# 160 tokens gathered in place of 128 in the expert stage of a two-block model, with dense products of 352 columns

## The reference, cut to what matters

```python
q = (hb @ wq).reshape(128, 8, 2, 128)                      # 8 heads, two halves
s = einsum('thsd,snd->thsn', q, subkeys)                   # 128 scores for each half
s1, i1 = top_k(s[:, :, 0], 16); s2, i2 = top_k(s[:, :, 1], 16)
sc, ci = top_k(s1[..., None] + s2[..., None, :], 16)       # 16 best of 256 pairs
idx = e1 * 128 + e2                                        # 8*16 = 128 experts of 16384 for each token
gate = softmax(sc)
act = gelu(einsum('td,thkd->thk', hb, u_tab[idx])) * gate
out = einsum('thk,thkd->td', act, v_tab[idx])
```

## Time and profile before

| what | value |
|---|---|
| median of 3 runs | 4420.25 us (4418.15 to 4424.22) |
| the profiled execution | 4425.3 us, its span 4423.5 us |
| TensorE busy | 4248.9 us, 96% |
| VectorE, ScalarE, GpSimd busy | 3004.6, 1804.8 and 1455.6 us (68%, 41%, 33%) |
| chain that ended last | PE 79%, DVE 11%, ACT 3%, issue 3%, POOL 2%, DMA 2% |

### The profile page before, as it was taken

How to read it: one execution, slowest core, us unless ns; L and a number is a source line. 1 busy time by engine, 2 the same in 40 slices (tenths; PEclk the granted TensorE clock), 3 DMA queues, 4 the chain that set the end, 5 groups by cost and what they waited for, 6 DMA issues and landing times.

```text
span 4423.5 us, 66804 instructions
## 1 busy us (share of the span) xinstructions
PE 4248.9 (96%) x26227; PEld 3705.3 (84%) x26227; DVE 3004.6 (68%) x5041; ACT 1804.8 (41%) x2815; POOL 1455.6 (33%) x992
## 2 busy tenths in 40 slices
PE   7979999999999999999999999999999999999998
PEld 5856755779999999999989877699889877877997
DVE  5866657559767868788778446488378544655873
ACT  4245421233335653333355355355255333324542
POOL 2044224314885437778621110212111110112121
PEclk8989999999999999999999999899999999999999
DMA  4133521224886789999923322133323232102332
GB/s 181 52 106 116 185 76 48 91 92 132 285 267 240 265 332 383 372 388 382 341 91 101 100 78 72 39 110 96 100 91 106 91 108 74 48 35 67 106 99 73
DMA packets 232192, 665.76 MB, mean 151 GB/s; under 512 B 22519, under 2 KB 88455, under 8 KB 229704
## 3 DMA queue, kind: packets, MB, share of 16 engines
q1 hardware_dynamic: 110528, 389.87, 26.3%
q0 software_dynamic: 38752, 142.90, 8.6%
q10 hardware_dynamic: 82600, 128.71, 8.2%
HBM read 593.24 MB, written 68.16 MB: 150 GB/s over the span
## 4 chain that ended last, share of the span: by engine, by line
PE 79%; DVE 11%; ACT 3%; issue 3%; POOL 2%; DMA 2%; ACTq 0%; DVEq 0%; POOLq 0%
PE ps L273 15%; PE ps L275 15%; PE ps L274 15%; PE ps L2732 5%; PE ps L2734 5%; PE ps L2733 5%; PE ps L1613 2%; PE ps L2326 2%; PE ps L3767 2%; PE ps L1692 1%; DVE r L242 1%; DVE r L292 1%; PE ps L405 1%; DVE A L904 1%; DMA A<-in_w_late 1%
## 5 line engine op out<-in xcount | busy, mean ns | idle before, releaser
L273 PE MATMUL ps<-r,r 128*128 128x384 f32 (+1 forms) x3944 | 1452.6, 368 | 14.0 <-POOL r L242 6.7
L275 PE MATMUL ps<-r,r 128*128 128x384 f32 (+1 forms) x3944 | 1435.2, 364 | 0.0
L274 PE MATMUL ps<-r,r 128*128 128x384 f32 (+1 forms) x3944 | 1434.9, 364 | 0.0
L236 ACT ACTIVATE r<-A 128x1024 fp32r<-128x1024 f32 x513 | 542.1, 1058 | 1177.0 <-PE ps L275 1031.0
L242 DVE TENSOR_TENSOR r<-A,r 128x1024 fp32r<-128x1024 f32 x401 | 511.3, 1277 | 728.1 <-ACT r L236 727.8
L273 PEld LDWEIGHTS ps<-r,r 128*128 128x128 f32 x3944 | 745.1, 189 | 108.2 <-issue 14.3
L274 PEld LDWEIGHTS ps<-r,r 128*128 128x128 f32 x3944 | 745.1, 189 | 81.8 <-issue 3.6
L275 PEld LDWEIGHTS ps<-r,r 128*128 128x128 f32 x3944 | 743.9, 189 | 81.2
L289 ACT ACTIVATE r<-A 128x512 fp32r<-128x512 f32 (+1 forms) x796 | 474.2, 611 | 509.4 <-DVE A L2418 242.9
L2732 PE MATMUL ps<-r,r 128*128 128x256 f32 x2128 | 601.0, 282 | 3.4 <-DVE A L2896 2.5
L2734 PE MATMUL ps<-r,r 128*128 128x256 f32 x2128 | 600.4, 282 | 0.0
(11 more groups left out here) (534 smaller groups left out, 5425.5 us busy)
## 6 DMA issues: line engine op xcount, KB each, us to landing
A<-in_pu SPq DMA_DIRECT2D x128, 512.0 KB, 4.1
A<-in_pv SPq DMA_DIRECT2D x128, 512.0 KB, 6.8
A<-in_f1i SPq DMA_DIRECT2D x88, 512.0 KB, 3.6
A<-in_f2i SPq DMA_DIRECT2D x88, 512.0 KB, 3.6
A<-in_w_in SPq DMA_DIRECT2D x48, 512.0 KB, 3.7
acts<-A ACTq DMA_DIRECT2D x128, 192.0 KB, 4.0
gates<-A ACTq DMA_DIRECT2D x8, 3072.0 KB, 11.1
A<-gates ACTq DMA_DIRECT2D x32, 768.0 KB, 10.3
```

What stands on the lines that cost most here:

```text
L236: a.activation(self.vr(self.wr0 + 2048 * (u % RW), 1024), self.v(self.st0 + 1024 * (u % RS), 1024), ACT.Copy).then_inc(*self.S.on("a", "hi ...
L273: t.matmul(o, hi, xh, start=first and k == k0, stop=False)
L274: t.matmul(o, hi, xl, start=False, stop=False)
L275: m = t.matmul(o, lo, xh, start=False, stop=final and k == K - 1)
```

## The change

NT becomes 352, and NG = 160 tokens are gathered. The 32 more can't have a partition each, so their 128 choices are shared by four groups of partitions: 32 more row steps, in which partitions 32q to 32q+31 hold the tokens 128 to 159 with a quarter of the choices each. For that the tokens are written four times by 32 small matmuls ("x again") in place of the copy XT, their choices and gates are moved by four small DMAs ("moved"), and at the end the four partial sums are added by a product with "fold", which is 32 columns wide now. There are 320 row steps: 66 in the choices in 27 small groups (48 in 9), 76 in the gates (28), 15 in later (14), 3 in the first x and the 160 of the table v over x = 5 to 121 (38 over x = 0 to 27, then 128 over x = 30 to 124). `ROWS` has eight gathers for seven units (before: 16 for 17). The gate steps are 88. L2355 reads its 128 constants in SBUF and no longer in PSUM; L2353 still reads them in PSUM. The core of the diff:

```diff
...
-UT, NT, LATER = 76, 384, 14
+UT, NT, LATER = 76, 352, 14
+NG, TG = 512 - NT, NT // 8
...
-        self.plan([("scores", n) for n in range(16)], (4, 5))
+        self.plan([("x again", 0), ("x again", 1)] + [("scores", n) for n in range(16)], (4, 5))
...
-        for at, m in ([(("choices", i), 16 * (i + 1) // 3) for i in range(9)] + [(("gates", i), 48 + 28 * (i + 1) // 96) for i in range(96)]
-                      + [(("later", r), 76 + r + 1) for r in range(LATER)]
-                      + [(("second", x), min(90 + 38 * (x + 1) // 28, 128) if x < 30 else 128 + min(128, 128 * (x - 29) // 95)) for x in range(128)]):
+        for at, m in ([(("choices", i), 66 * (i + 1) // 27) for i in range(27)] + [(("gates", i), 66 + 76 * (i + 1) // (NT // 4)) for i in range(NT // 4)]
+                      + [(("later", r), 142 + 15 * (r + 1) // LATER) for r in range(LATER)]
+                      + [(("second", x), min(157 + x + 1, NG) if x < 5 else NG + min(NG, NG * (x - 4) // 117)) for x in range(128)]):
...
-            row, c = self.v(L.ROWS + 1024 * (n % 6), 1024), n % 128
+            row, c = self.v(L.ROWS + 1024 * (n % 6), 1024), n % NG
...
-            if n < 128:
-                tokens = self.last2[:, :] if n < L.kept else self.v(L.XT, 1024)
+            if n < NG:
+                tokens = self.last2[:, :] if c < 128 else self.v(L.XT, 1024)
...
-            acc, w = self.v(L.ACC, 1024), self.v(L.COEF + c, 1)
+            acc, w = self.v(L.ACC if c < 128 else L.XT, 1024), self.v(L.COEF + c, 1)
...
     EXP, TURN = {13: 0, 32: 1, 50: 2, 69: 3}, {34: 1, 53: 2, 72: 3}
-    ROWS = {14 + 17 * n // 16: n for n in range(48)}
+    ROWS = {c: [n for n in range(66) if 14 + 7 * n // 8 == c] for c in range(UT)}
...
+                ps = self.bank_t(t, "x again", i)
+                for q in range(4):
+                    x = self.v(L.SC0 + 512 * (4 * i + q) + 128, NG - 128)
+                    for c in range(4):
+                        m = t.matmul(ps[32 * c:32 * c + 32, 128 * q:128 * q + 128], x, self.cst("ident"), start=True, stop=True)
+                m.then_inc(*S.on("t", "x again", i))
...
-            if o in (4, 8):
...
-                a.activation(self.v(L.XT + 512 * i, 512), self.ps("x tokens", i)[:, :], ACT.Copy).then_inc(*S.on("a", "out", "x tokens", i))
+            if o in (3, 4):
...
+                a.activation(self.v(L.XT + 512 * i, 512), self.ps("x again", i)[:, :], ACT.Copy).then_inc(*S.on("a", "out", "x again", i))
...
+                    a.wait_ge(*S.at("chosen again"))
+                    for q in range(4):
+                        a.dma_start(self.A[32 * q:32 * q + 32, L.GATE:L.GATE + 2 * NG].rearrange("p (s c) -> p s c", s=2)[:, :, 128:NG],
+                                    self.A[0:32, L.EX:L.EX + 256].rearrange("p (s c) -> p s c", s=2)[:, :, 32 * q:32 * q + 32]).then_inc(*S.dma("moved"))
...
+        if rows is not None:
+            self.rows_v(v, "choices", rows)
...
+        if rows is not None:
+            self.rows_v(v, "choices", rows + 1)
...
+        if rows is not None:
+            self.rows_v(v, "choices", rows + 2)
...
-            self.best_v(v, "pairs", tt, 8, 256, L.CA, L.CB, L.SV, ciu, None)
+            self.best_v(v, "pairs", tt, 8, 256, L.CA, L.CB, L.SV, ciu, None, 9 * tt - 9 if tt else None)
             if tt:
-                self.rows_v(v, "choices", 3 * tt - 3)
+                self.rows_v(v, "choices", 9 * tt - 6)
...
+                if tt:
+                    self.rows_v(v, "choices", 9 * tt - 5 + 2 * s)
...
-                if tt and s == 0:
-                    self.rows_v(v, "choices", 3 * tt - 2)
+                if tt:
+                    self.rows_v(v, "choices", 9 * tt - 4 + 2 * s)
...
             if tt:
...
-                self.rows_v(v, "choices", 3 * tt - 1)
...
+                self.rows_v(v, "choices", 9 * tt - 1)
...
-                v.tensor_scalar(a[:, q, :], self.PS[2][:, 0:128], e1[:, q:q + 1], gate[:, q:q + 1], ALU.is_equal, ALU.mult).then_inc(*(S.on("v", "one hot gated", b) if q == 7 else S.on("v")))
+                v.tensor_scalar(a[:, q, :], self.cst("iota128"), e1[:, q:q + 1], gate[:, q:q + 1], ALU.is_equal, ALU.mult).then_inc(*(S.on("v", "one hot gated", b) if q == 7 else S.on("v")))
...
-                t.wait_ge(*S.at("row used", 255))
-                for i in range(2):
+                t.wait_ge(*S.at("row used", 2 * NG - 1))
+                for i in range(3):
                     sm = self.bank_t(t, "sum t", i)
-                    for q in range(4):
-                        m = self.tr(t, sm[:, 128 * q:128 * q + 128], self.v(L.ACC + 512 * i + 128 * q, 128))
+                    for k in range(3 * i, min(3 * i + 3, 8)):
+                        at = NG * (k % 3)
+                        self.tr(t, sm[:, at:at + 128], self.v(L.ACC + 128 * k, 128))
+                        m = t.matmul(sm[:, at + 128:at + NG], self.v(L.XT + 128 * k, 128), self.cst("fold"), start=True, stop=True)
...
```

More of the change, by code:

```diff
@@ L614, in modtr_t @@
         for o in range(4):
-            m = t.matmul(self.PS[b][:, 2 * o:2 * o + 2], self.v(L.ROW + 512 * (n % 2) + 128 * o, 128), self.cst("fold"), start=True, stop=True)
+            m = t.matmul(self.PS[b][:, 2 * o:2 * o + 2], self.v(L.ROW + 512 * (n % 2) + 128 * o, 128), self.cst("fold", 0, 2), start=True, stop=True)
         m.then_inc(*S.on("t", "modtr", n))
@@ L1989, in lay_peer @@
         L.XT, L.ROWS, L.ACC = self.al(1024), self.al(6144), self.al(1024)
-        L.DOT, L.COEF, L.GATE, L.IDX = (self.al(128) for _ in range(4))
+        L.DOT, L.COEF, L.GATE, L.IDX = (self.al(NG) for _ in range(4))
         L.SP = self.al(4 * NT)
@@ L2005, in lay_peer @@
         self.plan([("q", o) for o in range(16)], range(4))
-        self.plan([("scores", n) for n in range(16)], (4, 5))
+        self.plan([("x again", 0), ("x again", 1)] + [("scores", n) for n in range(16)], (4, 5))
         L.bank = [c % 3 if c < L.THREE else (c + 1) % 2 for c in range(128)]
         for b in range(3):
-            self.plan([("early", c) for c in range(128) if L.bank[c] == b] + [("vsum", b)] + ([("sum t", b)] if b < 2 else []), (b,))
+            self.plan([("early", c) for c in range(128) if L.bank[c] == b] + [("vsum", b)] + [("sum t", b)], (b,))
         for b in range(3):
@@ L2064, in rows_a @@
         S, L = self.S, self.L3
-        if L.steps[at] and L.steps[at][-1] == 127:
-            a.wait_ge(*S.at("row used", 127))
-            a.activation(self.v(L.COEF, 128), self.v(L.DOT, 128), ACT.Gelu).then_inc(*S.on("a", "row acts"))
+        if L.steps[at] and NG - 1 in L.steps[at]:
+            a.wait_ge(*S.at("row used", NG - 1))
+            a.activation(self.v(L.COEF, NG), self.v(L.DOT, NG), ACT.Gelu).then_inc(*S.on("a", "row acts"))
     def topk_s(self, s):
@@ L2187, in topk_a, with best_v @@
                 a.wait_ge(*S.at("gate t", tt))
-                a.activation(self.v(L.ET, 3 * NT).rearrange("p (s t) -> p s t", s=3)[:, :, 128 * tt - 128:128 * tt],
-                             self.ps("gate t", tt)[:, 0:384].rearrange("p (s t) -> p s t", s=3), ACT.Copy).then_inc(*S.on("a", "out", "gate t", tt))
-    def best_v(self, v, what, tt, n, w, src, alt, val, idx, need):
+                lo = max(0, 128 * tt - NG)
+                a.activation(self.v(L.ET, 3 * NT).rearrange("p (s t) -> p s t", s=3)[:, :, lo:128 * tt + 128 - NG],
+                             self.ps("gate t", tt)[:, 0:384].rearrange("p (s t) -> p s t", s=3)[:, :, NG + lo - 128 * tt:128], ACT.Copy).then_inc(*S.on("a", "out", "gate t", tt))
+                if tt == 1:
+                    a.wait_ge(*S.at("chosen again"))
+                    for q in range(4):
+                        a.dma_start(self.A[32 * q:32 * q + 32, L.GATE:L.GATE + 2 * NG].rearrange("p (s c) -> p s c", s=2)[:, :, 128:NG],
+                                    self.A[0:32, L.EX:L.EX + 256].rearrange("p (s c) -> p s c", s=2)[:, :, 32 * q:32 * q + 32]).then_inc(*S.dma("moved"))
+                    S.mark("moved", "moved")
+    def best_v(self, v, what, tt, n, w, src, alt, val, idx, need, rows=None):
         S = self.S
@@ L2231, in topk_v @@
             v.wait_ge(*S.at("x tokens", i))
-            v.wait_ge(*S.at("out", "x tokens", i))
         v.wait_ge(*S.at("residual kept", "peer"))
@@ L2289, in topk_g @@
             self.weights_g(g, 8)
-            if c in self.ROWS:
-                if self.ROWS[c] == 0:
+            for n in self.ROWS[c]:
+                if n == 0:
                     g.wait_ge(*S.at("chosen"))
-                    g.wait_ge(*S.at("out", "x tokens", 1))
-                self.gather(g, self.ROWS[c])
+                    g.wait_ge(*S.at("out", "x again", 1))
+                self.gather(g, n)
     def gates_early(self, i):
@@ L2372, in gates_g @@
         S, L = self.S, self.L3
-        for n in range(48, 52):
+        for n in range(66, 70):
             self.gather(g, n)
@@ L2525, in sum_v @@
         S = self.S
-        h = self.v(self.HX + 512 * k, 128)
```

(7 more changed lines are left out.)

54 lines of the change are left out of this document (33 added, 21 removed).

## The result

The changed kernel is slower. Its median is 4439.6 us (4430.7 to 4450.8, 11 runs) against 4420.5 us (4409.0 to 4429.0) for the kernel before on the same chip, a ratio of 1.0038 with a 95% interval of 1.0028 to 1.0048. The forecast was 4376 us with a range to 4418. The profiled execution after took 4435.4 us (span 4433.6), before 4425.3 (span 4423.5).

What follows compares the result with a forecast made beforehand. TensorE, never resting in the expert layer, was taken as the bound, with VectorE, GpSimd and DMA nearly full. Added work 8, choices -21, gates -6, later and second -26 gave -45 us: 4376 us against the 4420.25 median, range 4332 to 4418.

Steps and rivals of the forecast that it cites:

- The gates: Gate stage: 44 blocks of 5.48 us make 241 us, a change of -6 us, with bounds of 223 and 304.
- the choices: Choices stage: -26 from narrower products, -6.7 from a wait removed, +12 of new waits, together -21 us.
- later and second: Second half: TensorE could save 48 us, but DMA holds units to 4.05 us, so 573 us instead of 599, -26.
- (a): Gates: L2355 reading SBUF was claimed to take 0.15 us a piece, 1.17 us for the eight of a block.
- (b): Gates: VectorE's L2355 pieces held up by GpSimd were claimed to lose 1.0 us a block, bounds 0 and 2.43.
- (c): Gates: VectorE's L2353 at 1.22 us and 1.73 rows of 1.21 us, 2.09 us, in each block.
- The term for PSUM: Gates: with L2355 still at 0.33 us a piece, VectorE would need 5.95 us a block, 262 us for the stage.
- The second rival: Gates: GpSimd's `lo` holds VectorE's L2355 series 2.4 us in each block; stage 304 us, +57, whole 4438 us; chance 0.14.
- The gain from the groups: Choices: nine small groups for three large ones per tt use slots more evenly, removing 6.7 us of TensorE's waiting.
- The narrower products: Choices: 32 columns fewer save TensorE 0.34 us in each of 76 units, -26 us.
- The bound: Second half: DMA engines limit the pace at a share of at most 1.04, 4.05 us a unit; TensorE alone needs 3.88.
- x again: Query stage: 64 records of 0.108 us counted one by one add 6.9 us, or 1.7 if they ran beside each other.

Runs made afterwards that it cites:

- experiment 3: The changed kernel with the 38 low parts (`lo`) in the gates written by VectorE instead of GpSimd: 4412.2 us, ratio 0.9978.
- experiment 1: The changed kernel with one edit undone, the eight tensor_scalar of a block reading their 128 constants in PSUM again: 4394.4 us, ratio 0.9935.
- experiment 5: The kernel before with only the small groups added, its 48 rows of the choices in 27 groups instead of 9: 4408.9 us, ratio 0.9974.
- Experiment 6: On experiment 1, the exponentials of tt = 2 and 3 two units later and their turns one later: 4390.2 us, ratio 0.9933.
- experiment 7: On experiment 1, 14 gathers moved from the choices to the gates (52 and 90 rows instead of 66 and 76): 4398.6 us, ratio 0.9956.
- experiment 4: The changed kernel with half of each 512 KB piece of table v left unloaded: 4415.6 us, ratio 0.9982.
- experiment 8: On experiment 1, the 15 rows of later moved, 8 to the gates and 7 to x = 0 to 4: 4408.8 us, ratio 0.9972.

## Why the prediction was wrong, step by step

From trace to trace the forecast was -45 us and the result +10. The gates miss by 49, the choices by 13, later and second by 12; the rest is 19 us better than forecast, which no step explains.

**The gates: this step failed.** The prediction put a piece of the series at 0.15 us and the time lost to GpSimd at 1.0 us a block, and so the block at 5.48 us and the stage at 241. The runs show a block of 6.59 us (290/44). By terms, for one block: (a) the free series of eight takes 2.05 us (experiment 3), 0.256 a piece; the prediction had 1.17. The 0.15 was worked out from an operation with other operands (L2247, 0.21 us), and it was wrong by 39 us over 44 blocks. In PSUM the same series takes 2.55, so the move to SBUF could win 0.5 us a block at best. (b) The series lost (161.1 - 44 * 2.05)/44 = 1.61 us a block, not 1.0: 27 us more. (c) The one-hot and the rows took what is left of 6.59, 2.93 us, not 3.3: 17 less; the prediction priced them by their durations of 1.22 and 1.21 us, and in the timeline above they start 1.13 to 1.14 apart. 39 + 27 - 17 is the 49 us between 241 and 290. The larger error was thus the free price, not the contention: with 0.256 a piece even the forecast's own 1.0 us gives 44 * (1.22 + 2.05 + 2.09 + 1.0) = 280 us, a kernel that is slower in the gates by 32. The term for PSUM was wrong too, in the other direction: 262 us was forecast if a piece stayed at 0.33, and experiment 1 ran the stage in 244.5.

**The second rival** named the mechanism, its place and nearly the time (4438), with a chance of 0.14. It was right by luck in the sum: it priced the hold at 2.43 us a block and the point from which it decides at 1.9 (by its own terms it is 2.0: 44 * (4.48 + 2.0) is 285 us, 38 above 247), and the hold came to 1.61. What made it decide at 1.61 was (a). Its argument, that GpSimd goes straight from a gather into a `lo`, is the row at 1512.91 above; 37 of the 44 series met a `lo`, where the prediction had 0.4 of them. The prediction read the pair of L2246 and `lo` as agreeing with the rule that the second to issue waits. The rows agree that one stands until the other ends, but not with that order: L2246 began at 1207.28 and the `lo` at 1207.46, the piece above at 1512.49 and its `lo` at 1512.91, and both times the one that began first stood.

**TensorE's clock** was no term of the prediction. After the wait of 3.16 us in the timeline below (start, us, line, idle us and releaser in brackets) the matmuls start 0.29 us apart and take 0.49, in a window whose granted clock is 0.79, and not the 0.16 and 0.32 of full speed; that is the lower of the two levels, 1.2 GHz in place of 2.4, for part of the window.

```profile
1497.14 1.31 PE L2359 MATMUL ps<-A 128*128 128x128 f32 x8 [3.16 <-DVE A L2388]
...
1500.02 0.49 PE L274 MATMUL ps<-r,r 128*128 128x352 f32 x1
1500.31 0.49 PE L275 MATMUL ps<-r,r 128*128 128x352 f32 x1
...
1501.77 0.33 PE L275 MATMUL ps<-r,r 128*128 128x352 f32 x1
1501.93 0.33 PE L276 MATMUL ps<-r,r 128*128 128x352 f32 x1
```

This is one of nine falls in the gates, each behind one or two waits of 2.1 to 3.2 us for the one-hots; the mean of the stage is 0.95, where it was 1.00 before. With VectorE busy 290 of 290 us the clock adds nothing to the gates' length by itself. TensorE shows 247.6 us of busy time for work that 44 * 5.07 = 223 would do. A mean of 0.95 means a tenth of the stage at half speed, which accounts for at most 15 of these 25 us.

**The choices** came to -7.9 in place of -21. The gain from the groups was right (experiment 5). The narrower products should have given 76 * (4.22 - 3.81) = 31 us more than the groups' 9.6, and the stage would be 294 us; it is 326, so 33 us of new losses took all of it, against 12 forecast. The waits of this stage, 1025 to 1352 us:

```profile
ACT r L237 <- DMA A<-in_pu: 76.8, 26, 5.7
...
ACT A L2196 <- DVE A L2291: 24.7, 4, 8.0
PE ps L274 <- POOL r L243: 12.3, 14, 2.1
PEld ps L274 <- ACT A L2104: 11.2, 4, 6.1
PEld ps L274 <- issue: 11.1, 12, 1.4
...
PE ps L274 <- ACT A L2104: 5.8, 1, 5.8
```

TensorE itself stood 19 of the 33 us. GpSimd's `lo` holds it for 12.3 us (forecast 9). The exponentials hold ScalarE for 24.7 us in four waits, and TensorE behind the gelu that follows for 5.8 us, once (forecast 3). The rows of PEld, the weight load, aren't to be added to that: its longest wait, 6.1 us, is the same stretch, and the three others fall into waits for a `lo`. So the waits came out at 19 for 12. The prediction had nothing for the other 14 us, in which TensorE works but more slowly. About 6 are the clock: the mean is 0.98, so 4% of 327 us at half speed. And about 7 are a second spacing of the products of 352 columns at full granted clock:

```profile
1120.10 0.33 PE L276 MATMUL ps<-r,r 128*128 128x352 f32 x1
...
1125.10 0.33 PE L276 MATMUL ps<-r,r 128*128 128x352 f32 x1
```

These are 30 products in 5.00 us, 166.7 ns each, with the clock at 1.00 from 1105 to 1150 us; from 1195 to 1215 us they come every 158.3 ns. The mean of the stage is 162.4. With 384 columns they come every 176 ns in all stages of the kernel before. What sets the spacing no run shows. Experiment 6 gave 12.8 us back by two places, experiment 7 gave 16.2 back by 14 fewer rows.

**Later and second** came to -13.6 in place of -26. The bound was the right one, the DMA engines (experiment 4), and their share of 1.03 was in the forecast's range. The unit took 4.10 us, not 4.05, for 6 us in all. The other 6 are in later, where 14 units took 62.5 us, 4.46 each. Most of it is one wait at its start:

```profile
1655.02 1.06 ACT L237 ACTIVATE r<-A 128x1024 fp32r<-128x1024 f32 x1 [9.14 <-DMA A<-in_pu]
...
1656.48 0.66 PE L274 MATMUL ps<-r,r 128*128 128x352 f32 x1 [4.50 <-ACT A L2104]
```

The load that ScalarE waited for was issued at 1641.44 and landed 13.6 us later, against a median of 4.7 in the gates, with the DMA engines at a share of 1.00 from 1642 to 1663 us; TensorE stood behind ScalarE, and its mean granted clock in that stretch is 0.84. A load is late in experiment 8 too, without rows. Which transfers delay it (a store of the gates, 2816 KB, was issued at 1640.78) no run tests, and it stays open. The two figures of the ceiling that the prediction set beside each other (the Trainium skill, "DMA: Bandwidth & Descriptors", Specifications) stand thus: the stretch from 1705 to 2195 us moved 385 GB/s, above 358, which is not the limit here, and below 435, which no run reached.

**The small terms.** Matmuls of 352 columns come 24 in 3.81 us (2103.65 - 2099.84), 158.7 ns each, in this stretch; forecast 161.7. "x again" was taken at 6.9 us, since its rows were to be counted one by one, and its lower bound of 1.7 was nearly right:

```profile
2099.84 0.32 PE L274 MATMUL ps<-r,r 128*128 128x352 f32 x1
...
2103.65 0.32 PE L274 MATMUL ps<-r,r 128*128 128x352 f32 x1
...
938.74 1.08 PE L2151 MATMUL ps<-A 128*32 128x128 f32 x32
939.75 0.50 PE L274 MATMUL ps<-r,r 128*128 128x512 f32 x1
```

32 records in 1.01 us from start to start, 2 us for both halves.

## What to carry to other kernels

Before an operand moves from PSUM to SBUF on VectorE, look at what GpSimd does at that time and at how much of its time VectorE has left: in this kernel the same edit cost nothing with 18% of VectorE's time free and 45 us with none. A short operation needs a price from a row of the same form and the same operands; 39 of the 49 us by which the gates missed came in with a neighbour's 0.21 us. And when a change holds several edits, price the one that is least needed apart: here the rest of it, without that edit, was worth 26 us.

## What the runs showed of the hardware

- A tensor_scalar of 128 x 128 fp32 with two scalars from memory comes every 0.256 us with its input in SBUF and every 0.318 us with it in PSUM. The one in SBUF stands until the end of a GpSimd tensor_tensor of 2.4 us that it meets (up to 3.2 us for one piece), also where it began 0.4 us before it; the one in PSUM doesn't stand at all (426 ns at most). That the two exclude each other is what the Trainium skill says ("SBUF — State Buffer", Who interferes with whom); its order, whoever issues first, is not that of the recorded starts. The runs put the number to it for a series of eight: 2.05 us free, 3.97 us when met.
- The DMA engines held a share of 1.03 and 385 GB/s for 490 us, with gathers, loads of 512 KB and pieces of 176 and 704 KB mixed.
- Four products of 32 rows each, written to four groups of 32 columns, ran beside each other: 32 records in 1.01 us, where records on all 128 columns take 0.108 us each, 3.5 us for 32.
- TensorE's clock fell to its lower level nine times in the gates of the changed kernel, each time behind one or two waits of 2.1 to 3.2 us, and the stage had a mean of 0.95; in experiment 1, with 12.3 us of these waits in place of 41.7, it had 0.99.
- Products of 352 columns came every 158.3 ns in some stretches and every 166.7 ns in others, all at a granted clock of 1.00, in one kernel and one stage; those of 384 columns came every 176 ns throughout.
